# Gate projections as one 512-column product, halves summed on VectorE, mixer order planned anew

## The reference, cut to what matters

```python
u = rmsnorm(h, norm_mix_w)                     # (272, 1024)
p = u @ w_in                                   # pool 1024 | q,k,v 3x1024 | z 1024 | a 8 | b 8 | gates 2x1024
A = pooling mixer(p_pool)                      # windows 2/4/8/16, a 256x256 product in each of 4 groups
B = gated DeltaNet(conv(q,k,v), a, b)          # 8 heads x 128, chunked; o = rmsnorm(o) * silu(z)
h = h + (sigmoid(g_A) * A + sigmoid(g_B) * B) @ w_out
h = h + hierarchical_moe(rmsnorm(h))           # 32 SwiGLU experts in 4 groups, 2 of one group per token
out = rmsnorm(h)[:, 16:]
```

## Time and profile before

| | us |
|---|---|
| median of 3 runs | 781.25 (780.7 to 785.59) |
| the profiled execution, its own time | 781.17 |
| its span | 779.4 |
| PE busy in the span | 749.0 |
| DVE busy in the span | 323.2 |
| ACT busy in the span | 312.1 |

### The profile page before, as it was taken

The page is one execution under the profiler, slowest core; times in us unless marked ns, Lnnn a source line. Parts: engine busy times, 40 slices in busy tenths (PEclk is TensorE's granted clock), DMA queues, the critical chain, the costliest instruction groups (busy, mean ns, idle before and its releaser), DMA issues.

```text
span 779.4 us, 16087 instructions
## 1 busy us (share of the span) xinstructions
PE 749.0 (96%) x6517; PEld 535.0 (69%) x6517; DVE 323.2 (41%) x794; ACT 312.1 (40%) x632; POOL 124.6 (16%) x208
## 2 busy tenths in 40 slices
PE   8999999999999999899999999999999988998895
PEld 7989989998999988655655555555556555455452
DVE  4784787688575855811311211221113112112012
ACT  6876678576684744712221221212122211111113
POOL 7473242225433640000000000000000000000000
PEclk9999999999999999999999999999999999999999
DMA  8537555564754568999999999999999999999992
GB/s 205 145 85 183 154 143 130 136 150 114 186 137 125 160 192 320 375 380 430 428 426 428 426 428 430 425 427 425 430 427 427 427 427 425 428 430 426 427 409 96
DMA packets 81104, 241.06 MB, mean 309 GB/s; under 512 B 6913, under 2 KB 65394, under 8 KB 68994
## 3 DMA queue, kind: packets, MB, share of 16 engines
q1 hardware_dynamic: 80722, 239.19, 80.7%
q10 hardware_dynamic: 304, 0.79, 0.4%
HBM read 238.92 MB, written 1.05 MB: 308 GB/s over the span
## 4 chain that ended last, share of the span: by engine, by line
PE 75%; DMA 11%; DVE 6%; issue 5%; POOL 2%; ACT 1%; DVEq 0%; POOLq 0%; ACTq 0%
PE banks L2143 23%; PE banks L1798 18%; PE banks L2199 12%; DMA ring<-in_expert_w_up_dram 10%; PE banks L2075 3%; PE banks L2154 3%; PE banks L1993 2%; PE banks L2175 1%; DVE desk L1367 1%; PE banks L1930 1%; PE banks L1917 1%; DVE rounded L1316 1%; PE banks L1934 1%; PE banks L1955 1%; PE banks L1978 1%
## 5 line engine op out<-in xcount | busy, mean ns | idle before, releaser
L2143 PE MATMUL banks<-ring,bench 128*64 128x256 f32 x2048 | 240.0, 388 | 11.6 <-DMA ring<-in_expert_w_up_dram 7.7
L2143 PEld LDWEIGHTS banks<-ring,bench 128*64 128x64 f32 x2048 | 146.2, 134 | 112.8 <-issue 23.1
L1798 PE MATMUL banks<-rounded 128*128 128x256 f32 (+3 forms) x1344 | 197.5, 293 | 1.4 <-DVE rounded L1328 1.0
L1798 PEld LDWEIGHTS banks<-rounded 128*128 128x128 f32 (+1 forms) x1344 | 170.1, 187 | 5.4 <-POOL rounded L1192 1.2
L1697 DVE TENSOR_TENSOR bench<-banks,bench 128x256 f32<-128x256 f32 x32 | 13.6, 425 | 263.0 <-PE banks L2143 172.1
L2199 PE MATMUL banks<-ring,bench 128*64 128x512 f32 x512 | 116.9, 598 | 0.5 <-ACT bench L1081 0.5
L1092 ACT ACTIVATE ysb<-banks 64x512 f32<-64x512 f32 x63 | 37.2, 591 | 147.1 <-PE banks L2199 146.3
L2199 PEld LDWEIGHTS banks<-ring,bench 128*64 128x64 f32 x512 | 33.9, 136 | 63.2 <-issue 60.1
L860 ACT ACTIVATE rounded<-room 128x1024 fp32r<-128x1024 f32 x64 | 67.4, 1054 | 22.5 <-PE banks L1798 15.0
L1081 ACT ACTIVATE bench<-banks 128x256 f32<-128x256 f32 x32 | 12.3, 384 | 148.1 <-PE banks L2175 148.1
L1316 DVE TENSOR_TENSOR rounded<-room,rounded 128x1024 fp32r<-128x1024 f32 x49 | 61.2, 1249 | 15.4 <-ACT rounded L860 14.3
(11 more groups left out here) (309 smaller groups left out, 858.3 us busy)
## 6 DMA issues: line engine op xcount, KB each, us to landing
ring<-in_expert_w_gate_dram SPq DMA_DIRECT2D x30, 2048.0 KB, 29.0
ring<-in_expert_w_down_dram SPq DMA_DIRECT2D x30, 2048.0 KB, 27.8
ring<-in_expert_w_up_dram SPq DMA_DIRECT2D x29, 2048.0 KB, 29.2
room<-in_w_in_dram SPq DMA_DIRECT2D x56, 512.0 KB, 4.4
ring<-in_expert_w_gate_dram SPq DMA_DIRECT2D x8, 512.0 KB, 5.9
ring<-in_expert_w_up_dram SPq DMA_DIRECT2D x8, 512.0 KB, 6.5
ring<-in_expert_w_down_dram SPq DMA_DIRECT2D x8, 512.0 KB, 18.3
room<-in_w_out_dram SPq DMA_DIRECT2D x8, 512.0 KB, 4.4
```

The source lines that it names most:

```text
L1798: ins = T.matmul(o, a, b[:, k, lo_at:L], start=(k == 0 and n == 0), stop=(k == KT - 1 and n == 2))
L2143: ins = T.matmul(pb[5 + c][half * 64:half * 64 + SLOTS, 0:256], xgT[:, q % ROOMS, kt, j * SLOTS:(j + 1) * SLOTS], w[:, kt, half], start=(k ...
```

## The change

For the tiles of z, gB and gA (24 of the 56) a step k issues two products and not three. `uhi` and `ulo` become two halves of one tensor `uboth` at the same addresses. The first product multiplies `whi` by both halves, 2 x 256 moving columns, and fills a whole bank (columns 0 to 255 for uhi, 256 to 511 for ulo). The second, wlo x uhi, adds 256 columns to the first half. A new step `join` on DVE sums the two halves with a TENSOR_REDUCE of 128 x 256 pairs from the bank into `zs`, `thB` or `thA`. ACT then applies Silu or Tanh in place in SBUF, and frees the bank as before. The waits for room in `zs`, `thB` and `thA` move from ACT to DVE with it, and ACT waits for the new semaphore `joined`.

In the plan a step of such a tile costs 0.324 (0.355 before), `join` costs 0.6 on DVE, `PERIOD`, `SHIFT` and `HEAD_SHIFT` have new values, and `LO_BEHIND` is gone. So the order of all engines in the mixer stage is another. `TILE_ORDER`, `POOL_LO` and everything behind the mixers stay.

```diff
@@ -105,23 +105,23 @@
 PIECE_AT = {n: (i // 4, i % 4) for i, n in enumerate(range(FIRST_PIECE, FIRST_PIECE + 12 * PIECE_STEP, PIECE_STEP))}
 POOL_PARTS = 4
 POOL_LO = {0} | {n for n, (t, j) in enumerate(TILES) if t in ("P", "gA") and 5 <= n < len(TILES) - 2}
-LO_BEHIND = [(("lo", 10), ("tf", 0, 3)), (("lo", 34), ("tf", 4, 1))]
-PERIOD = 39.9
+JOINED = ("z", "gB", "gA")
+PERIOD = 42.2
 CLOSE = 4
 TURN = 3.1
 LEVEL = 0.31
 TURN_OVER = 0.09
 STAY = 5.3
 SHIFT = {
-    "mixhi": -0.8, "mixlo": -28.5, "round": 7.1, "lo": 1.2, "proj": 1.1, "take": 8.7, "taps": -3.7, "silu": 15.9, "zg": -23.7,
-    "window": -12.1, "m": -3.3, "mix": -33.4, "gam": -2.9, "rel": -5.2, "darg": -1.8, "dexp": 8.0, "sq": 4.5, "nn": 7.1,
-    "norm": -71.8, "dm": 6.3, "G": 7.7, "KT": 3.0, "VT": 2.8, "ab": -1.4, "base": 8.4, "qkdt": -1.0, "kb": -2.6,
-    "kd": 1.7, "mask": -2.0, "W": -0.6, "wb": 8.6, "YT": 0.8, "uc": 5.5, "u": 9.3, "wT": 1.8, "ue": 4.3,
-    "we": 6.4, "sb": -8.8, "so": 0.5, "sa": 11.3, "vn": 11.0, "ort": 34.1, "orec": -4.6, "oT": 15.9, "uhi": -6.3,
-    "ulo": -15.1, "abp": 0.9, "abT": -3.5, "abt": 12.7, "xa": -10.0, "axp": 3.8, "aln": 12.7, "beta": -10.9, "gamp": -7.9,
-    "skb": -5.8,
+    "mixhi": 28.8, "mixlo": 75.2, "round": 9.4, "lo": -8.0, "proj": 12.8, "take": 19.4, "taps": 3.7, "silu": 33.8,
+    "zg": 24.8, "window": -119.4, "m": 33.3, "mix": -179.0, "gam": -142.9, "rel": 15.8, "darg": -141.5, "dexp": -18.4,
+    "sq": 44.3, "nn": -67.9, "norm": -69.8, "dm": -94.3, "G": -107.7, "KT": 7.7, "VT": -35.1, "ab": 5.7,
+    "base": -32.8, "qkdt": -87.5, "kb": 38.1, "kd": -11.5, "mask": 81.5, "W": -124.7, "wb": 24.3, "YT": -38.2,
+    "uc": 55.8, "u": 11.0, "wT": -75.2, "ue": -20.3, "we": -82.4, "sb": -26.4, "so": -7.1, "sa": -55.7, "vn": -27.0,
+    "ort": 70.1, "orec": 92.1, "oT": 32.9, "uhi": -32.5, "ulo": -22.4, "abp": 11.0, "abT": 62.0, "abt": -157.9,
+    "xa": 80.2, "axp": -61.0, "aln": -49.5, "beta": -7.1, "gamp": -76.9, "skb": 168.3,
 }
-HEAD_SHIFT = [-9.0, 6.6, 0.0, -1.8, -5.3, 0.0, 2.6, 7.0]
+HEAD_SHIFT = [26.6, 13.2, 19.5, 18.5, 6.2, -3.2, 2.6, 16.8]
 
 SILU, EXP, SQRT = "silu", "exp", "sqrt"
 
@@ -162,7 +162,7 @@
             if n == 0:
                 op(("proj", n, k), "pe", 0.24, when(("round", n) if k == 0 else ("proj", n, k - 1), ("ulo", k)), -49 + k, gets=("proj", n) if k == 0 else None)
             else:
-                op(("proj", n, k), "pe", 0.364 if t == "q" else 0.38 if wide else 0.355, when(("lo", n) if k == 0 else ("proj", n, k - 1), project_end(n - 1) if k == 0 else None), d - 3 + 0.3 * k,
+                op(("proj", n, k), "pe", 0.364 if t == "q" else 0.38 if wide else 0.324, when(("lo", n) if k == 0 else ("proj", n, k - 1), project_end(n - 1) if k == 0 else None), d - 3 + 0.3 * k,
                    gets=("proj", n) if k == 0 else None)
         if n == 0:
             op(("projlo",), "pe", 1.0, when(("proj", n, 7), ("lo", n)), -40)
@@ -174,12 +174,15 @@
             op(("silu", t, j), "act", 0.42, when(("taps", n), ("sb", j - 4, 2) if j >= 4 else None, ("silu", "kqv"[(i - 1) % 3], j - (i == 0)) if j or i else None),
                d + 2, table=SILU)
         if t == "z":
-            op(("take", n), "act", 0.37, when(pr, ("out", j - 2) if j >= 2 else None), d, frees=[("proj", n)], table=SILU)
+            op(("join", n), "dve", 0.6, when(pr, ("out", j - 2) if j >= 2 else None), d)
+            op(("take", n), "act", 0.37, when(("join", n)), d, frees=[("proj", n)], table=SILU)
         if t == "gB":
-            op(("take", n), "act", 0.37, when(pr, ("zg", j - 1) if j else None), d, frees=[("proj", n)], table="tanh")
+            op(("join", n), "dve", 0.6, when(pr, ("zg", j - 1) if j else None), d)
+            op(("take", n), "act", 0.37, when(("join", n)), d, frees=[("proj", n)], table="tanh")
             op(("zg", j), "dve", 0.45, when(("take", n), ("take", TILE_OF["z", j]), ("zg", j - 1) if j else None), d)
         if t == "gA":
-            op(("take", n), "act", 0.37, when(pr, ("mix", j // 2 * 2 - 1) if j >= 2 else None), d, frees=[("proj", n)], table="tanh")
+            op(("join", n), "dve", 0.6, when(pr, ("mix", j // 2 * 2 - 1) if j >= 2 else None), d)
+            op(("take", n), "act", 0.37, when(("join", n)), d, frees=[("proj", n)], table="tanh")
         if t == "P":
             g = j // 2
             op(("take", n), "act", 0.37, when(pr, ("window", g * 2 - 1) if j >= 2 else None), d, frees=[("proj", n)])
@@ -400,9 +403,7 @@
 
 
 SEQ_OF, WHERE, USES, _, _, _ = plan()
-for _lo, _behind in LO_BEHIND:
-    SEQ_OF["dve"].remove(_lo)
-    SEQ_OF["dve"].insert(SEQ_OF["dve"].index(_behind) + 1, _lo)
+JOIN_AT = {step[1]: n + 1 for n, step in enumerate(s for s in SEQ_OF["dve"] if s[0] == "join")}
 OT_AT = {step[1:]: n + 1 for n, step in enumerate(s for s in SEQ_OF["pool"] if s[0] == "mask")}
 TF_AT = {step[1:]: n + 1 for n, step in enumerate(s for s in SEQ_OF["dve"] if s[0] == "tf")}
 MIXHI_AT = {step[1]: n + 1 for n, step in enumerate(s for s in SEQ_OF["act"] if s[0] == "mixhi")}
@@ -469,8 +470,8 @@
 
         win = room[:, 0:WIN_SLOTS * D].rearrange("p (s k c) -> p s k c", s=WIN_SLOTS, k=KT)
 
-        uhi = take_rounded(KT * L).rearrange("p (k t) -> p k t", k=KT)
-        ulo = take_rounded(KT * L).rearrange("p (k t) -> p k t", k=KT)
+        uboth = take_rounded(2 * KT * L).rearrange("p (u k t) -> p u k t", u=2, k=KT)
+        uhi, ulo = uboth[:, 0], uboth[:, 1]
         wabhi = take_rounded(KT * 16).rearrange("p (k n) -> p k n", k=KT)
         wablo = take_rounded(KT * 16).rearrange("p (k n) -> p k n", k=KT)
         wlo = take_rounded(HI_SLOTS * D).rearrange("p (s c) -> p s c", s=HI_SLOTS)
@@ -860,7 +861,10 @@
                 nc.scalar.activation(whi[:, n % HI_SLOTS], win[:, n % WIN_SLOTS].rearrange("p k c -> p (k c)"), ACT.Copy).then_inc(S("whi"), 1)
 
             def take_tile(n, t, j):
-                p = filled(act, ("proj", n))
+                if t in JOINED:
+                    act.wait_ge(S("joined"), JOIN_AT[n])
+                else:
+                    p = filled(act, ("proj", n))
                 if t in "kqv":
                     i = LIST[t]
                     col = {"q": 0, "k": 8, "v": 16}[t] + j
@@ -869,17 +873,11 @@
                         act.wait_ge(S("silu"), 3 * (j - 1) + i + 1)
                     nc.scalar.activation(acc[:, i, FROM[t]:L], p[:, 0:L - FROM[t]], ACT.Copy, scale=w3).then_inc(S("tap3"), 1)
                 elif t == "z":
-                    if j >= 2:
-                        taken(act, ("oT", j - 2))
-                    takes(nc.scalar.activation(zs[:, j % 2, :], p[:, 0:SEQ], ACT.Silu), ("proj", n))
+                    takes(nc.scalar.activation(zs[:, j % 2, :], zs[:, j % 2, :], ACT.Silu), ("proj", n))
                 elif t == "gB":
-                    if j >= 1:
-                        act.wait_ge(S("zg"), j)
-                    takes(nc.scalar.activation(thB[:, :], p[:, 0:SEQ], ACT.Tanh, scale=0.5), ("proj", n))
+                    takes(nc.scalar.activation(thB[:, :], thB[:, :], ACT.Tanh, scale=0.5), ("proj", n))
                 elif t == "gA":
-                    if j >= 2:
-                        act.wait_ge(S("mixed"), j // 2 * 2)
-                    takes(nc.scalar.activation(thA[:, j % 2, :], p[:, 0:SEQ], ACT.Tanh, scale=0.5), ("proj", n))
+                    takes(nc.scalar.activation(thA[:, j % 2, :], thA[:, j % 2, :], ACT.Tanh, scale=0.5), ("proj", n))
                 else:
                     if j >= 2:
                         act.wait_ge(S("pooled"), j // 2 * 2)
@@ -1372,6 +1370,22 @@
                             ins.then_inc(S("conv"), 1)
                             dve.wait_ge(S("conv"), 3 * j + i + 1)
                             dve.sem_inc(free[WHERE[("proj", n)][0]], 1)
+                if kind == "join":
+                    t, j = TILES[step[1]]
+                    p = filled(dve, ("proj", step[1]))
+                    if t == "z":
+                        if j >= 2:
+                            taken(dve, ("oT", j - 2))
+                        o = zs[:, j % 2, :]
+                    elif t == "gB":
+                        if j >= 1:
+                            dve.wait_ge(S("zg"), j)
+                        o = thB[:, :]
+                    else:
+                        if j >= 2:
+                            dve.wait_ge(S("mixed"), j // 2 * 2)
+                        o = thA[:, j % 2, :]
+                    V.tensor_reduce(o, p.rearrange("p (u t) -> p t u", u=2), AX.X, ALU.add).then_inc(S("joined"), 1)
                 if kind == "zg":
                     j = step[1]
                     taken(dve, ("proj", TILE_OF[("gB", j)]))
@@ -1823,7 +1837,12 @@
                     bank(pe, ("proj", n))
                 p = pb[WHERE[("proj", n)][0]]
                 lo = FROM.get(t, META)
-                ins = parts(p[:, 0:L - lo], whi[:, n % HI_SLOTS, k * P:(k + 1) * P], wlo[:, lo_slot(n), k * P:(k + 1) * P], k, lo)
```

(6 more changed lines are left out.)

## The result

The changed kernel took 791.3 us in the median of 8 runs (784.5 to 794.1), the kernel before 781.9 us (780.6 to 785.6). The ratio is 1.010 with an interval of 1.0073 to 1.0126: slower, by some 8 us. The profiled execution was the fastest of the eight: 784.5 us, span 782.8 us.

What follows compares the result with a forecast made beforehand. PE was taken to set the mixers' pace, DVE once for some 30 us, and DMA the expert stage; 781.2 us - 1.4 (products) + 2.8 (joins) + 0 (waits) + 0 (order) = 782.6 us, range 772 to 793.

Steps and rivals of the forecast that it cites:

- slower rival: Mixer stage: VectorE bounds more stretches, about half of the joins in tight places; +11.7 us, so 792.9 us; chance 0.24.
- likeliest case: Whole kernel: +1.4 us, so 782.6 us, own range 777 to 788; chance 0.42 together with its neighbour at 784.0.
- the quarter and the fifth: Shares of the faster outcome (near 775 us) and of the slower rival that stay within 1% of no change.
- Part 1, products: PE, mixer stage: two products for three, step 0.357 to 0.3495 us, saving 1.4 us; bounds -1.4 to +6.0 us.
- Part 2, joins: DVE, mixer stage: 24 joins of 0.692 us, four on the path at 160 to 190 us, costing 2.8 us.
- Part 3, waits: DVE and ACT, mixer stage: new wait for the product taken as 0, ACT's extra 1.0 us hidden.
- Bank and detour: Mixer stage: a bank is held some 0.7 us longer, but banks aren't short; 0.
- Part 4, the order: All engines, mixer stage: the new list order taken as 0, bounded by 4.8 us won or lost.
- The second stage: Expert stage behind the mixers: a stream of fixed length, untouched, so a shift of the mixers' end passes one to one.

Runs made afterwards that it cites:

- old_order_no_join: The kernel before with its old lists and the 512-column products, no join, ACT reading the first 256 columns of the bank: 782.2 us, ratio 1.001.
- old_order_joined: The kernel before with its old lists, but the 512-column products and the joins of the change: 790.9 us, ratio 1.0124.
- join_aside: Old lists, 512-column products, ACT reading the bank directly; at each join's place VectorE waits and runs a reduce nobody waits for: 791.7 us, ratio 1.0122.
- old_products: The changed kernel's new lists with the products and takes of the kernel before, no join executed: 784.0 us, ratio 1.0017.
- measured_plan: The changed kernel with measured durations in its plan (0.352 per step, 0.7 per join) and due times searched anew, no pauses: 788.3 us, ratio 1.0076.

## Where the prediction held and where it failed

The range (772 to 793) held the time, by luck more than by the working: 791.3 us lies in its last 2 us, and the range was that wide only for the slower rival. The direction of my likeliest case was right, but its size wasn't: +1.4 us forecast, +6.5 to +9.4 measured in two sets of runs, and both medians (791.3 and 788.4) lie outside its own 777 to 788. The slower rival came nearer in size, 792.9 us, for partly other reasons. My chances don't follow exactly from their cases either: the quarter and the fifth give 0.16, 0.65 and 0.19, where I wrote 0.17, 0.61 and 0.22.

- **Part 1, products.** 0.3495 us per step forecast, 0.35 measured; the plan's 0.324 isn't there. I put the 1.4 us on the path. `old_order_no_join` had about 1 us less than the kernel before in half of its runs and 2 to 4 more in the others, so nothing in the median.
- **Part 2, joins.** The duration was right (0.692 for 0.685). The step that failed is that only the four joins of 160 to 190 us "are on the path and 20 joins are hidden by PE": 2.8 us forecast, 9 us measured at unchanged lists (`old_order_joined` against `old_order_no_join`), and at most 2.2 us of it near the place where I had put it. I took the busy shares and the chain of waits as a map of which engine is short at each moment. But in the mixers PE's overlapping records cover its waits, as I had written myself. The likely reason, argued and not shown step by step: the chain runs through PE's filling products where the step that holds up the head's next level is on VectorE, and a list in fixed order passes each delay on.
- **Part 3, waits.** "I take 0" for the new wait on the product: VectorE stood idle 6.4 us before joins. `join_aside` has this wait and the time together, so its own share is open. Bank and detour were put at nothing; by the estimate at `join_aside` they can have cost some 2 us.
- **Part 4, the order.** Bounded by ±4.8 us, measured +2.1 in the medians (`old_products`). My argument that the lists were laid out for a lighter VectorE fits, and isn't shown: `measured_plan` without the other cures was no clear gain, with 27 us at the low clock in its profile.
- **What wasn't in the forecast at all** is the clock. All rows of before have 1.00, and I treated it as given. With the new lists PE idles 2.5 us once at 41 us and 1 to 1.5 us a few times later, and stretches of 3.4 to 17 us at 1.2 GHz follow in some executions. By the mean clocks that is the difference between the profiled 784.5 us and the four slowest of the eight runs (791.8 to 794.1); the run of 790.8 us isn't explained by it.
- **The second stage** has the same length (453.3 and 453.4 us), and the shift passed on one to one.

The Trainium skill ("TensorE: Matmul & The Clock Gate", A second HAM failure mode: psum-queue depth-cycling) describes PE idling shortly between groups of products often enough for its clock to fall and rise, and a throughput that suffers by it. The traces agree in kind: the clock falls and rises here too, at idle times of at most 2.5 us, and between the two profiles of the changed kernel 0.57 us was lost for each us at the low clock.

## What to carry to other kernels

In a hand-ordered pipeline where VectorE and ScalarE are some 70 to 80% busy, work moved to one of them is not hidden because another engine's records are at 96%. Here about half of it was paid (9 of 16 us); charge that much unless an experiment shows less. Look at the granted clock of several runs before a change that thins the feed of PE, and fill an unavoidable idle time with useless products if the clock falls behind it. A plan that is searched against durations is only as good as they are; and the profile of a single execution can miss most of the loss (3.4 of 9 us here).

## What the runs showed of the hardware

- A VectorE operation on three columns ended only with the last of four GpSimd operations that were issued without a wait between them, after 3.08 us; with a semaphore wait between them it took 0.69 us. The Trainium skill ("SBUF — State Buffer", SBUF: two separate sides) says that a GpSimd operation and a VectorE one in a 2-port mode, or with two SBUF inputs, share a pair of ports, that the one that starts first has the pair for its whole instruction, and that the other blocks. The trace agrees that VectorE's operation stood while GpSimd ran, but it stood over four instructions and not one. Why isn't shown.
- In 11 of the 14 profiles the clock was at half for 3.4, 6.8, 10.2 or 17.1 us at a time, each time behind an idle time of PE of 0.4 to 2.5 us. (The last microseconds of the expert stage, where PE has ended, aren't counted.) Most idle times of that length don't bring it: the kernel before stood 0.8 us at 56.7 us, the changed kernel 1.5 us at 138 us and `old_products` 2.5 us at 41 us, and all kept their clock there. Which one does differs between executions of the same program.
- Ten useless products of 128 columns in an idle time of 2.5 us made the changed kernel faster by 4 us or more.
